# Delta-rule solve: one direction's diagonal blocks made by VectorE transposes, one direction's far half evicted by VectorE, ScalarE's copies reordered

## The chip, the cores and the metric

One core of one Trainium2 chip runs the whole program. The metric is the device time of one execution in microseconds (us), lower is better.

## The reference, cut to what matters

The program is one inference step of a two-layer hybrid backbone: SwiGLU blocks and, between them, a token mixer of attention heads, RWKV-7 heads and retention heads. The change touches the RWKV-7 part alone: a scan over tokens in two directions, four heads of width 64, with a generalised delta rule:

```python
def rwkv7_scan(r, w, kk, kka, k, v, s0):
    def step(S, inp):
        r_t, w_t, kk_t, kka_t, k_t, v_t = inp
        sa = jnp.einsum('bzhvk,bzhk->bzhv', S, -kk_t)
        S = S * w_t[..., None, :] + sa[..., None] * kka_t[..., None, :] + v_t[..., None] * k_t[..., None, :]
        return S, jnp.einsum('bzhvk,bzhk->bzhv', S, r_t)
```

There are 512 latent tokens (started from a given state) and 128 context tokens (started from zero).

## The kernel before, in words

All tokens (640) stand in five chunks of 128: chunks 0 to 3 are latent, chunk 4 (`last`, `c == NL`) is the context. The scan of a chunk is turned into a triangular system per head and direction, and `solve(c)` solves it. Both directions (d = 0 and 1) and four heads go side by side. Each layer runs `solve(0)` to `solve(4)`, so there are ten solves in the program, eight of them not the last of their layer.

A solve inverts the 128x128 unit triangle in steps. First its four 32x32 diagonal blocks: `horner` and three `levels` work on compact tiles `Xc[d]` (128 partitions x 4 heads x 32 columns: block q of every head lies on partitions 32q to 32q+31) and on `XTc[d]`, the same with each 32x32 block transposed (L2062, VectorE). Then the pairs of 32-blocks: TensorE multiplies for the off-diagonal blocks (L1677, whose result ScalarE copies out as `T1` in L1918, then L1687, semaphore `dx_mm` with count 5c+4). The 64x64 diagonal triangles are then put together in `XT[d]` (128 x 4 heads x 128), which holds the transposed inverse, from two sources: the diagonal 32x32 blocks out of `XTc` (direction 0: ScalarE, `diagonal`, L1891; direction 1: VectorE, L2140, four copies of 32 partitions x 128 elements each) and the off-diagonal blocks, transposed out of PSUM by VectorE for both directions (L2148, two for direction 0, then two for direction 1). TensorE then multiplies `XT[d]` with the right-hand sides `R` (L1455, eight matmuls in each direction); half of `R` is the values, which ScalarE copies from PSUM in `values_out` (L1876, semaphore `lv`). ScalarE copies the result to `X` (L1929). The other half of the triangle follows: TensorE forms its product with the near half (L1710, semaphore `t1_mm` with count 5c+5), the product is copied from PSUM to `Zs[d]` (L1936: both directions on ScalarE, 64 partitions x 512 elements each), TensorE multiplies it (L1722, semaphore `gh_mm`), and VectorE adds it to `X` (L2163).

The order of the work on each engine is written out by hand, and the parts of the next chunk's preparation, `prep(c+1, 0)` to `prep(c+1, 4)`, are put between the steps of the solve. Each engine takes its own list in order, and waits on semaphores. Around the change the orders in a chunk that is not the last are:

- TensorE: L1677, `lk_values(c, 0)` (L1461), L1687, `lk_values(c, 1)` (L1461), L1455, `prep(c+1, 2)` (transposes L1407 and L1408, waiting for `alpha` and `kappa`), L1710, `prep(c+1, 3)` (transposes L1416 to L1419, which wait for `beta` and `rk` before the first of them), L1722, then `inner(c+1, 0, d)` (L1448), then the final products of chunk c.
- VectorE: the last level, L2140, L2148, `prep(c+1, 2)` (L2008 to L2011, gives `alpha`), `prep(c+1, 3)` (L2014 to L2025, gives `rho`, `beta` and `rk`), `prep(c+1, 4)` (L2036 to L2040, waits for `tok_T`, which the last of L1419 gives), L2163.
- ScalarE: `T1` twice (L1918), `values_out(c, 0)`, `diagonal(c)` (L1891), `values_out(c, 1)`, `X` twice (L1929), `Zs` twice (L1936), `prep(c+1, 3)` (L1819, L1822, wait for `tok_T`).
- GpSimd: four masks and the products of the preparation (L2262, L2251), with no step of its own in this stretch.

TensorE's `inner(c+1, 0, d)` waits for what `prep(c+1, 4)` of VectorE and `prep(c+1, 3)` of ScalarE put out (`beta_tok`, `v_tok`, `bv`, `alpha_tok`, `kappa_tok`).

In the last chunk there is no preparation; in its place `beside(...)` does the group norm and gate of earlier tokens: VectorE has `beside(3)`, `beside(4)`, `beside(5)` between L2148 and L2163, ScalarE has `beside(3)` between `diagonal` and `X`, `beside(4)` between `X` and `Zs`, and TensorE `beside(3)` ahead of L1455, `beside(4)` ahead of L1710, `beside(5)` ahead of L1722.

The semaphore of `t10` and `t11` (counts of `T1`, `X` and `Zs` of direction 0 and 1, six each in a chunk) is one for both directions, counted in turn:

```python
series("level_lx_out", 30, "t10", "t11")
```

Of the kernel before, what the change touches and what calls it, by code (L numbers as in the profile page):

```python
# [22 lines left out]
ACT = mybir.ActivationFunctionType  # L23
AX = mybir.AxisListType.X

P = 128
# [73 lines left out]
def flip(c):  # L100

    return 4 * (c % 2)
# [33 lines left out]
def build(nc, i, o):  # L136
    ctx = ExitStack()
    with ctx:
# [70 lines left out]
        PS = ctx.enter_context(nc.psum_tensor("PS", [P, 8, 512], F32))  # L209
# [113 lines left out]
        class Stage:  # L323
# [6 lines left out]
            def value(self, l, k):  # L330
# [103 lines left out]
        XT = [keep(f"XT{d}", [P, NH, P], rq) for d in range(2)]  # L434
# [3 lines left out]
        Zs = [keep(f"Zs{d}", [P, NH, P], fo) for d in range(2)]  # L438
# [15 lines left out]
        Xc, T1, XTc = ([place(f"{one}{d}", [P, NH, QUAD], at_lvl + 4 * P * (7 * d + at)) for d in range(2)]  # L454
                       for at, one in ((2, "Xc"), (3, "T1_"), (4, "XTc")))
# [10 lines left out]
        S = {}  # L466

        def stage(name, per):
            S[name] = Stage(ctx.enter_context(nc.semaphore(name)), per)

        def series(name, per, *names):
            s_ = ctx.enter_context(nc.semaphore(name))
            for turn, one in enumerate(names):
                S[one] = Stage(s_, per, turn, len(names))
# [52 lines left out]
        series("horner", 15, "b_mm0", "b_mm1")  # L527
        series("lak_v", 5, "lv0", "lv1")
        series("level_lx", 25, "t1_mm0", "t1_mm1")
        series("level_lx_out", 30, "t10", "t11")  # L530
        series("solve_results", 5, "gh_mm0", "gh_mm1", "fin_mm0", "fin_mm1", "yl_mm0", "yl_mm1")
        series("gh_out", 5, "gh0", "gh1")
        series("yl", 5, "yl_out0", "yl_out1")
# [10 lines left out]
        def until(eng, l, name, k):  # L544

            if S[name].per * l + k > 0:
                eng.wait_ge(S[name].sem, S[name].value(l, k))
# [1277 lines left out]
        def rwkv_scalar(a_, l):  # L1825
            until(a_, l, "pv", 40)
            until(a_, l, "s_mm", 40)
            until(a_, l, "mix_stored", 48)

            def prep(c, part):  # L1830

                prep_scalar(a_, l, c, part)

            def beside(lv):

                t = lv - 2
                if 0 <= t < NL:
                    gn_square(a_, l, NT + t)
                    gate_copy(a_, l, t, 0)
                if 0 <= t < 3:  # L1840
                    until(a_, l, "cols_T", t + 1)
                    if t == 0:
                        until(a_, l, "tok_T", 5)
                        until(a_, l, "rk", 5)
                        until(a_, l, "kd", 5)
                    cols = slice(t * P, (t + 1) * P)
                    a_.activation(act[0][:, 0:4, cols], PS[:, 2, :].rearrange("p (k t) -> p k t", k=4), ACT.Copy)
                    a_.activation(act[0][:, 6:8, cols], PS[:, 3, 0:256].rearrange("p (k t) -> p k t", k=2), ACT.Copy)\
                        .then_inc(S["cols_out"].sem, 1)
                if lv > 4:  # L1850
                    rwkv_columns(a_, l, lv - 5)

            def rows_out(c):

                for d in range(2):
                    until(a_, l, f"lb_mm{d}", c + 1)
                    until(a_, l, f"yl_mm{d}", max(c - 1, 0))
                    for pr in range(2):
                        m = a_.activation(LB[c % 2][d][:, pr:NH:2, :, :],
                                          PS[:, (4 + 2 * d + pr) ^ flip(c), :].rearrange("p (f e t) -> p f e t", f=2, e=2),  # L1860
                                          ACT.Copy)
                    m.then_inc(S[f"lb{d}"].sem, 1)

            def key_rows_out(c, d):

                until(a_, l, f"lk_mm{d}", c + 1)
                until(a_, l, f"yl_mm{d}", c)
                for pr in range(2):
                    m = a_.activation(LK[d][:, pr:NH:2, :, :],
                                      PS[:, (2 * d + pr) ^ flip(c), :].rearrange("p (f e t) -> p f e t", f=2, e=2), ACT.Copy)  # L1870
                m.then_inc(S[f"lko{d}"].sem, 1)

            def values_out(c, d):

                until(a_, l, f"lv_mm{d}", c + 1)
                a_.activation(R[c % 2][d][:, :, HD:P], PS[:, (2 + d) ^ flip(c), 0:DR].rearrange("p (h v) -> p h v", h=NH),  # L1876
                              ACT.Copy).then_inc(S[f"lv{d}"].sem, 1)

            def local_out(c, d):

                until(a_, l, f"yl_mm{d}", c + 1)
                a_.activation(Yls[:, c, d * DR:(d + 1) * DR], PS[:, (5 + 2 * d) ^ flip(c), 0:DR], ACT.Copy)\
                    .then_inc(S[f"yl_out{d}"].sem, 1)

            def diagonal(c):

                until(a_, l, "x0", 10 * c + 10)
                until(a_, l, "gh_mm0", c)
                for q in range(4):
                    at = slice(q * QUAD, (q + 1) * QUAD)  # L1890
                    m = a_.activation(XT[0][at, :, at], XTc[0][at, :, :], ACT.Copy)  # L1891
                m.then_inc(S["xt0"].sem, 1)

            def solve(c):
                f, last = flip(c), c == NL
                rows_out(c)
                if c == 0:
                    prep(0, 3)
                else:
                    local_out(c - 1, 0)  # L1900
                if not last:
                    prep(c + 1, 0)
                if c:
                    local_out(c - 1, 1)
                key_rows_out(c, 0)
                key_rows_out(c, 1)
                if not last:
                    prep(c + 1, 1)
                    prep(c + 1, 2)
                else:  # L1910
                    values_out(c, 0)
                    values_out(c, 1)
                    beside(1)
                    beside(2)
                for d in range(2):
                    until(a_, l, f"t1_mm{d}", 5 * c + 4)
                    until(a_, l, f"dx_mm{d}", 5 * c + 3)
                    a_.activation(T1[d][:].rearrange("p h t -> p (h t)"), PS[:, (4 + 2 * d) ^ f, 0:P], ACT.Copy)\  # L1918
                        .then_inc(S[f"t1{d}"].sem, 1)
                if not last:  # L1920
                    values_out(c, 0)
                diagonal(c)
                if last:
                    beside(3)
                else:
                    values_out(c, 1)
                for d in range(2):
                    until(a_, l, f"dx_mm{d}", 5 * c + 5)
                    a_.activation(X[d][:].rearrange("p h t -> p (h t)"), PS[:, (5 + 2 * d) ^ f, :], ACT.Copy)\  # L1929
                        .then_inc(S[f"t1{d}"].sem, 1)  # L1930
                if last:
                    beside(4)
                for d in range(2):
                    until(a_, l, f"t1_mm{d}", 5 * c + 5)
                    b = slice(64, P) if d == 0 else slice(0, 64)
                    a_.activation(Zs[d][b, :, :].rearrange("p h t -> p (h t)"), PS[b, (4 + 2 * d) ^ f, :], ACT.Copy)\  # L1936
                        .then_inc(S[f"t1{d}"].sem, 1)
                if last:
                    beside(5)
                    beside(6)  # L1940
                    local_out(c, 0)
                    local_out(c, 1)
                else:
                    prep(c + 1, 3)

            for c in range(NT):
                solve(c)
            rwkv_columns(a_, l, 2)
# [96 lines left out]
        def rwkv_vector(v_, l):  # L2045
            mm_ = lambda name, k: until(v_, l, name, k)
# [3 lines left out]
            def prep(c, part):  # L2050

                prep_vector(v_, l, c, part)
# [47 lines left out]
            def solve(c):  # L2100
                last = c == NL
# [35 lines left out]
                mm_("x1", 10 * c + 10)  # L2137
                for q in range(4):
                    at = slice(q * QUAD, (q + 1) * QUAD)
                    m = v_.tensor_copy(XT[1][at, :, at], XTc[1][at, :, :])  # L2140
                m.then_inc(S["xt1"].sem, 1)
                for d in range(2):
                    mm_(f"dx_mm{d}", 5 * c + 4)
# [6 lines left out]
                if last:  # L2150
                    beside(3)
                    beside(4)
                    beside(5)
                else:
                    prep(c + 1, 2)
                    prep(c + 1, 3)
                    prep(c + 1, 4)
                for d in range(2):
# [10 lines left out]
            def beside(lv):  # L2169

                if lv >= 3:
                    rwkv_gate(v_, l, lv - 3)
                if 2 <= lv <= 5:
                    gn_squares(v_, l, NT + lv - 2)
                if lv <= NL:
                    rwkv_centre(v_, l, lv - 1)
# [1073 lines left out]
```

## Time and profile before

| | us |
|---|---|
| median of 3 runs | 3168.57 |
| lowest and highest of them | 3167.96, 3171.4 |
| the profiled execution's own time | 3171.75 |
| its span in the profile | 3169.9 |
| TensorE busy | 3023.3 (95%) |
| VectorE busy | 1830.3 (58%) |
| ScalarE busy | 1078.5 (34%) |
| GpSimd busy | 412.2 (13%) |
| mean granted TensorE clock | 0.974 |

The mixer's ten solves lie in two stretches of the span, from 866 to 1057 us (layer 0) and from 2397 to 2613 us (layer 1). In the rows, a time is the start in us from the span's start, the next number how long it lasted; PE is TensorE's matmuls, PEld its weight loads, DVE VectorE, ACT ScalarE, POOL GpSimd, PS the PSUM; L and a number is the line of the kernel. The text in square brackets is the time that the engine sat idle before, and what ended it.

### The profile page before, as it was taken

The numbers are of one execution on the slowest core, as the hardware profiler recorded it, in microseconds if no ns is written. First come the engines' busy times: TensorE is split into PE (matmuls) and PEld (weight loads), VectorE is DVE, ScalarE is ACT, GpSimd is POOL, SyncE is SP. The second block draws the span as 40 slices with busy tenths as digits, with TensorE's granted clock in tenths as the row PEclk, the third lists the DMA queues.
The fourth block names the chain that finished last, engine by engine and source line by source line (L and its number), as shares of the span: only waits on it lengthen the run. The fifth ranks groups of instructions, "written<-read, shape, count | busy, mean of one in ns | idle before, by whom it ended". The sixth has DMA issues, their size and how long they took to land.

```text
span 3169.9 us, 62838 instructions
## 1 busy us (share of the span) xinstructions
PE 3023.3 (95%) x26760; PEld 2713.3 (86%) x26760; DVE 1830.3 (58%) x2648; ACT 1078.5 (34%) x1619; POOL 412.2 (13%) x465
## 2 busy tenths in 40 slices
PE   6999999999988899999999999999998879999998
PEld 5999978986777699998799998789776767999986
DVE  3767555666766666674656674633666676222235
ACT  3111254235433441113531113532454435211134
POOL 1000111002233220001100001110033233000100
PEclk8999999999899899999999999999998989999999
DMA  5344334311000233433433433432010003111134
GB/s 221 133 159 159 119 134 147 123 41 33 24 3 13 102 119 146 159 146 120 146 137 141 159 146 124 143 106 83 17 47 7 7 24 140 67 72 74 60 125 167
DMA packets 62635, 324.09 MB, mean 102 GB/s; under 512 B 8752, under 2 KB 12400, under 8 KB 42992
## 3 DMA queue, kind: packets, MB, share of 16 engines
q1 hardware_dynamic: 62448, 321.39, 27.7%
q8 instruction: 143, 2.34, 0.3%
q14 instruction: 44, 0.36, 0.0%
HBM read 318.05 MB, written 3.31 MB: 101 GB/s over the span
## 4 chain that ended last, share of the span: by engine, by line
PE 84%; DVE 7%; DMA 3%; ACT 2%; issue 2%; POOL 0%; SPq 0%; ACTq 0%; DVEq 0%; POOLq 0%
PE PS L2464 47%; PE PS L2547 17%; PE PS L2475 3%; DMA wo<-in_wo 2%; PE PS L695 2%; PE PS L1469 2%; DVE wo_lo L2864 1%; PE PS L719 1%; ACT wo_hi L2661 1%; PE PS L1448 1%; PE PS L1455 1%; PE PS L642 1%; DMA wm<-in_wm 1%; PE PS L707 1%; PE PS L1461 1%
## 5 line engine op out<-in xcount | busy, mean ns | idle before, releaser
L2464 PE MATMUL PS<-h_hi,wi_hi 128*128 128x384 f32 (+1 forms) x3360 | 799.7, 310 | 11.0 <-issue 11.0
L2464 PE MATMUL PS<-h_lo,wi_hi 128*128 128x384 f32 (+1 forms) x3360 | 797.7, 309 | 0.0
L2464 PE MATMUL PS<-h_hi,wi_lo 128*128 128x384 f32 (+1 forms) x3360 | 797.7, 309 | 0.0
L2464 PEld LDWEIGHTS PS<-h_hi,wi_hi 128*128 128x128 f32 x3360 | 526.6, 188 | 14.0 <-issue 13.2
L2464 PEld LDWEIGHTS PS<-h_lo,wi_hi 128*128 128x128 f32 x3360 | 526.4, 188 | 0.7
L2464 PEld LDWEIGHTS PS<-h_hi,wi_lo 128*128 128x128 f32 x3360 | 526.4, 188 | 0.7
L2547 PE MATMUL PS<-wo_hi,a_hi 128*128 128x512 f32 x968 | 394.5, 408 | 21.7 <-DVE wo_lo L2864 14.6
L2864 DVE TENSOR_TENSOR wo_lo<-wo,wo_hi 128x1024 fp32r<-128x1024 f32 x208 | 256.1, 1232 | 259.5 <-ACT wo_hi L2661 258.5
L2654 ACT ACTIVATE sg<-PS 128x640 f32<-128x640 f32 x88 | 62.2, 706 | 937.5 <-PE PS L2464 937.5
L2547 PE MATMUL PS<-wo_lo,a_hi 128*128 128x512 f32 x968 | 378.9, 391 | 0.0
L2547 PE MATMUL PS<-wo_hi,a_lo 128*128 128x512 f32 x968 | 378.7, 391 | 0.0
L2290 DVE SCALAR_TENSOR_TENSOR macc<-wm,csil,macc 128x512 f32<-128x512 f32 x448 | 337.0, 752 | 15.9
L2661 ACT ACTIVATE wo_hi<-wo 128x1024 fp32r<-128x1024 f32 x208 | 220.3, 1059 | 342.2 <-PE PS L2547 226.9
L2858 DVE TENSOR_TENSOR act<-sg,PS 128x256 f32 (+3 forms) x176 | 78.0, 485 | 431.8 <-ACT sg L2654 431.8
L2850 DVE TENSOR_TENSOR wi_lo<-wi,wi_hi 128x2048 fp32r<-128x2048 f32 x112 | 256.4, 2290 | 79.5 <-ACT wi_hi L2648 79.3
L2547 PEld LDWEIGHTS PS<-wo_hi,a_hi 128*128 128x128 f32 x968 | 182.3, 188 | 84.6 <-DVE wo_lo L2864 34.4
L2648 ACT ACTIVATE wi_hi<-wi 128x2048 fp32r<-128x2048 f32 x112 | 213.5, 1906 | 11.4 <-DMA wi<-in_wi 8.7
L2547 PEld LDWEIGHTS PS<-wo_lo,a_hi 128*128 128x128 f32 x968 | 182.7, 189 | 39.4 <-issue 4.8
L2547 PEld LDWEIGHTS PS<-wo_hi,a_lo 128*128 128x128 f32 x968 | 182.6, 189 | 39.2
L3050 POOL TENSOR_TENSOR gcol<-modc,ngc 128x16 f32<-128x16 f32 x6 | 2.5, 412 | 1199.6 <-PE PS L2464 594.8
L2872 DVE TENSOR_TENSOR a_lo<-act,a_hi 128x512 fp32r<-128x512 f32 (+1 forms) x98 | 79.4, 811 | 43.7 <-ACT a_hi L2678 43.7
L3024 POOL TENSOR_SCALAR stat<-stat 128x1 f32<-128x1 f32 x60 | 24.8, 414 | 614.0 <-ACT PS L2684 576.0
(323 smaller groups left out, 3841.1 us busy)
## 6 DMA issues: line engine op xcount, KB each, us to landing
wi<-in_wi SPq DMA_DIRECT2D x88, 1024.0 KB, 4.9
wo<-in_wo SPq DMA_DIRECT2D x176, 512.0 KB, 3.5
wm<-in_wm SPq DMA_DIRECT2D x36, 2048.0 KB, 7.4
wi<-in_win SPq DMA_DIRECT2D x24, 1024.0 KB, 5.2
wo<-in_wout SPq DMA_DIRECT2D x32, 512.0 KB, 3.5
wq<-in_wq SPq DMA_DIRECT2D x2, 1024.0 KB, 4.8
out_y_sample<-x SPq DMA_DIRECT2D x4, 512.0 KB, 4.7
lvl<-in_lvl SPq DMA_DIRECT2D x2, 896.0 KB, 6.0
```

The source lines that it names most:

```text
L695: mm = pe.matmul(dst, q, KT[0:96, h, a:z], start=True, stop=True)
L1469: mm = pe.matmul(PS[at, bank, h * QUAD:(h + 1) * QUAD], lhs(h, at), rhs(h, at), start=True, stop=True)
L2290: a = dve.scalar_tensor_tensor(out=macc[:, z, :], in0=w[:, k, :], scalar=csil[:, k, z:z + 1], in1=macc[:, z, :], op0=ALU.mult, op1=ALU.add)
L2464: mm = pe.matmul(PSF[0:cols, at:at + GW[g]], st, h[g][:, k, :], start=(k == 0 and q == 0), stop=(k == KD - 1 and q == 2))
L2475: mm = pe.matmul(PS[:, 3 * j + t // 2, (t % 2) * 256:(t % 2 + 1) * 256], h[g][:, k, at], w[:, j, k, :], start=(k == 0 and q == 0), stop=(k ...
L2547: mm = pe.matmul(PS[:, OUT_BANK[t] + half, :], a, w[:, (V0(n) + b) % 2, kk, :], start=(u == 0 and kk == 0 and q == 0), stop=True, skip_gro ...
L2648: act_.activation(wi_hi[:, j, :, :], wi[:, j, :, :], ACT.Copy).then_inc(s_wih, 1)
L2661: act_.activation(wo_hi[:, V % 2, :, :], wo[:, V % 2, :, :], ACT.Copy).then_inc(s_woh, 1)
L2850: dve.tensor_tensor(wi_lo[:, j, :, :], wi[:, j, :, :], wi_hi[:, j, :, :].bitcast(F32), ALU.subtract).then_inc(s_wil, 1)
L2858: a = dve.tensor_tensor(tile_at(act[g], f), sg[:, j, GA[g]:GA[g] + GW[g]], PSF[:, up:up + GW[g]], ALU.mult)
L2864: dve.tensor_tensor(wo_lo[:, V % 2, :, :], wo[:, V % 2, :, :], wo_hi[:, V % 2, :, :].bitcast(F32), ALU.subtract).then_inc(s_wol, 1)
L2872: dve.tensor_tensor(act_lo(g, A, b == 0), act[g][:, 2 * u:2 * u + 2, :], act_hi(g, A, b == 0).bitcast(F32), ALU.subtract).then_inc(s_al, 1)
```

## The change

Three edits. VectorE's four copies `XTc[1]` to `XT[1]` become four transposes of `Xc[1]` to `XT[1]` (a 32x32 block transpose gives the same blocks). The eviction of the product to `Zs[1]` goes from ScalarE to VectorE, where it stands behind `prep(c+1, 2)` and ahead of `prep(c+1, 3)`, with a wait for `t1_mm1` (in the last chunk behind `beside(4)` and ahead of `beside(5)`); `t10` and `t11` get a semaphore each. On ScalarE `values_out(c, 0)` goes behind `diagonal(c)` in chunks that are not the last.

```diff
@@ -527,7 +527,8 @@
-        series("level_lx_out", 30, "t10", "t11")
+        stage("t10", 30)
+        stage("t11", 30)
@@ -1917,12 +1918,11 @@
                     a_.activation(T1[d][:].rearrange("p h t -> p (h t)"), PS[:, (4 + 2 * d) ^ f, 0:P], ACT.Copy)\
                         .then_inc(S[f"t1{d}"].sem, 1)
-                if not last:
-                    values_out(c, 0)
                 diagonal(c)
                 if last:
                     beside(3)
                 else:
+                    values_out(c, 0)
                     values_out(c, 1)
@@ -1930,11 +1930,9 @@
                 if last:
                     beside(4)
-                for d in range(2):
-                    until(a_, l, f"t1_mm{d}", 5 * c + 5)
-                    b = slice(64, P) if d == 0 else slice(0, 64)
-                    a_.activation(Zs[d][b, :, :].rearrange("p h t -> p (h t)"), PS[b, (4 + 2 * d) ^ f, :], ACT.Copy)\
-                        .then_inc(S[f"t1{d}"].sem, 1)
+                until(a_, l, "t1_mm0", 5 * c + 5)
+                a_.activation(Zs[0][64:P, :, :].rearrange("p h t -> p (h t)"), PS[64:P, 4 ^ f, :], ACT.Copy)\
+                    .then_inc(S["t10"].sem, 1)
@@ -2137,7 +2135,7 @@
                 mm_("x1", 10 * c + 10)
                 for q in range(4):
                     at = slice(q * QUAD, (q + 1) * QUAD)
-                    m = v_.tensor_copy(XT[1][at, :, at], XTc[1][at, :, :])
+                    m = v_.transpose(XT[1][at, :, at], Xc[1][at, :, :])
                 m.then_inc(S["xt1"].sem, 1)
@@ -2150,9 +2148,15 @@
                 if last:
                     beside(3)
                     beside(4)
+                else:
+                    prep(c + 1, 2)
+                mm_("t1_mm1", 5 * c + 5)
+                mm_("gh_mm1", c)
+                v_.tensor_copy(Zs[1][0:64, :, :].rearrange("p h t -> p (h t)"), PS[0:64, 6 ^ flip(c), :])\
+                    .then_inc(S["t11"].sem, 1)
+                if last:
                     beside(5)
                 else:
-                    prep(c + 1, 2)
                     prep(c + 1, 3)
                     prep(c + 1, 4)
```

## Rows read from the trace of the kernel before

**Rows 1.** The page: busy share of each engine, and the chain that ended last.
```profile
PE 3023.3 (95%) x26760; PEld 2713.3 (86%) x26760; DVE 1830.3 (58%) x2648; ACT 1078.5 (34%) x1619; POOL 412.2 (13%) x465
...
PE 84%; DVE 7%; DMA 3%; ACT 2%; issue 2%; POOL 0%; SPq 0%; ACTq 0%; DVEq 0%; POOLq 0%
```
**Rows 2.** Longest pieces of that chain within 866 to 1090 us: start, us, what.
```profile
919.87 1.21 DVE XT L2140
922.05 3.13 PE PS L1455 x16
...
927.63 0.59 PE PS L1416 x4
...
930.61 2.00 PE PS L1448 x16
```
**Rows 3.** Timeline of VectorE in chunk 1 of layer 0.
```profile
917.29 0.31 DVE L2062 STREAM_TRANSPOSE XTc<-Xc 128x128 f32<-128x128 f32 x1
...
918.23 3.10 DVE L2140 COPY XT<-XTc 32x128 f32<-32x128 f32 x4
921.35 1.30 DVE L2148 STREAM_TRANSPOSE XT<-PS 32x128 f32<-32x128 f32 x4
...
923.57 0.68 DVE L2014 TENSOR_TENSOR E<-E,rwz 128x512 f32<-128x512 f32 x1
...
925.58 0.61 DVE L2025 SCALAR_TENSOR_TENSOR rk<-rk,mcol,rwz 128x128 f32<-128x128 f32 x2
928.77 0.69 DVE L2036 COPY btok<-PS 128x512 f32<-128x512 f32 x1 [2.58 <-PE PS L1419]
929.38 0.41 DVE L2038 COPY vtok<-PS 128x256 f32<-128x256 f32 x1
```
**Rows 4.** Timeline of GpSimd in the same chunk.
```profile
916.04 2.50 POOL L2262 TENSOR_TENSOR LB<-LB,mask 128x512 f32<-128x512 f32 x2
918.49 2.51 POOL L2262 TENSOR_TENSOR LK<-LK,mask 128x512 f32<-128x512 f32 x2
```
**Rows 5.** Instructions on the tile XT: ns min/median/max; below, who waited (us, times).
```profile
L2140 DVE COPY XT<-XTc x40: 206/864/1220, 882.2 to 2588.2; 32x128 f32<-32x128 f32 x40
...
  PE PS L1455: 16.0, 7
```
**Rows 6.** Timeline of TensorE in the same chunk.
```profile
919.34 0.69 PE L1461 MATMUL PS<-vtok,LK 128*64 128x64 f32 x16
922.05 3.13 PE L1455 MATMUL PS<-R,XT 128*128 128x128 f32 x16 [2.02 <-DVE XT L2148]
...
927.57 0.66 PE L1416 MATMUL PS<-ident,ab 128*128 128x128 f32 x4
```
**Rows 7.** Timeline of ScalarE in the same chunk.
```profile
918.32 0.28 ACT L1918 ACTIVATE T<-PS 128x128 f32<-128x128 f32 x1 [0.24 <-PE PS L1677]
...
919.21 1.25 ACT L1891 ACTIVATE XT<-XTc 32x128 f32<-32x128 f32 x4
920.48 0.38 ACT L1876 ACTIVATE R<-PS 128x256 f32<-128x256 f32 x1
...
927.67 1.21 ACT L1936 ACTIVATE Zs<-PS 64x512 f32<-64x512 f32 x2 [1.85 <-PE PS L1710]
```
**Rows 8.** Stretches of 2 us: busy us of each engine; PEclk is the third number from the end.
```profile
922.00:924.00 2.00, 1.95 (x12) 1.96 (x13) 1.90 (x6) 0.49 (x1) 0.00 (x0) 0.70 0.00 0
924.00:926.00 2.00, 2.00 (x11) 2.00 (x11) 1.89 (x5) 0.70 (x2) 0.00 (x0) 0.50 0.00 0
926.00:928.00 2.00, 2.00 (x25) 1.66 (x24) 0.19 (x1) 0.33 (x1) 0.00 (x0) 0.95 0.00 0
```
**Rows 9.** Timeline of VectorE in the last chunk of layer 0.
```profile
1043.41 0.75 DVE L2202 TENSOR_TENSOR Yls<-Yls,PS 128x256 f32<-128x256 f32 x2 [1.58 <-PE PS L1747]
...
1045.73 0.68 DVE L1049 TENSOR_TENSOR yc<-yc,gst 128x512 f32<-128x512 f32 x1
...
1048.88 1.40 DVE L2163 TENSOR_TENSOR X<-X,PS 64x512 f32<-64x512 f32 x2
```

## The prediction

> **What bounds the kernel now.** I read the page first: TensorE is busy for 95% of the span, and the chain that ended last is 84% TensorE and 7% VectorE [rows 1]. That says only that work off this chain is free, so I next read the chain inside the solves [rows 2]. There VectorE's copies into `XT` (L2140) stand on the chain right ahead of TensorE's L1455, and from L1455 on the chain stays on TensorE: L1407/L1408, L1710, and, without a gap, L1416. So two places count: what TensorE waits for at L1455, and what it would wait for at L1416.
>
> At L1455 the view of instructions on the tile gives the size: TensorE waited 16.0 us in 7 of the ten solves for `XT` [rows 5]. The timelines of chunk 1 tell why. TensorE's L1461 started at 919.34 and its 0.69 us end at 920.03; L1455 starts at 922.05 after 2.02 idle [rows 6]. VectorE took 3.10 us for four copies of 32 x 128, and only then came to L2148 [rows 3]. One such copy takes 0.21 us at best, 0.86 in the median, 1.22 at worst [rows 5], and GpSimd was at its masks, 1.25 us each, from 916.04 to 921.00 [rows 4]. The worst copy is about one mask long: the copies are held up beside GpSimd. A VectorE transpose of 128 x 128 at 917.29, beside the same masks, took 0.31 [rows 3, 4]. The Trainium skill (GPSIMD Engine Reference, Specifications) says that GpSimd shares its SBUF interface with VectorE instructions that run in a two-port mode or read two SBUF inputs; by that a plain fp32 copy is exposed and a transpose need not be, and the trace agrees (0.86 against 0.31).
>
> **Part 1, transposes for copies.** Four transposes of 32 partitions out of PSUM take 1.30 us, 0.33 from start to start [rows 3]. With an SBUF source the nearest row is 0.31. Ends: 1.30, if that holds; 3.10, if these are held up like the copies. I take 1.3. In chunk 1: transposes from 918.23 to 919.5, then L2148, whose direction 0 (two transposes) is done at about 920.2.
>
> **Part 2, ScalarE's order.** L1455 of direction 0 also waits for `values_out(c, 0)`. Its new place is behind `diagonal`: the second `T1` starts at 918.32, `diagonal` follows at about 918.6 and takes 1.25, then `values_out` 0.38 [rows 7], done at 920.25. That is beside VectorE's 920.2, so L1455 can start at 920.3 in place of 922.05. Of the 2.02 idle some 0.2 to 0.3 stays. Over the seven waits: 16.0 minus 7 x 0.2 is **14.6 us gained**, all in chunks that are not the last (the eighth of them had no wait there: TensorE itself came late).
>
> **Part 3, the eviction on VectorE.** This adds a wait to VectorE, and I ask what is queued behind it. VectorE's `prep(c+1, 3)` runs from L2014 at 923.57 to the end of L2025 at 926.19: 2.62 us [rows 3]. TensorE's L1416 needs `beta` and `rk`, which these give, and starts at 927.57 [rows 6]: before, they were ready 1.4 us early. Now VectorE waits for L1710 first, evicts, and only then starts them. And L1710 is the step right ahead of L1416 on TensorE; L1722, which uses `Zs`, is queued behind L1416. So TensorE must wait, once L1710 is done, for
> - the hand-over to VectorE, 0.04 (L1710 ended at 927.63 [rows 2], ScalarE's copy started at 927.67 [rows 7]);
> - the eviction. Nearest rows: a PSUM copy of 128 x 512 on VectorE, 0.69 with the next starting 0.61 later [rows 3]; ScalarE needs 1.21 for two [rows 7]. I take 0.61;
> - `prep(c+1, 3)`: 2.62;
> - the hand-over to TensorE, 0.1.
>
> Together 3.37 us in each of eight chunks, **27.0 us lost**. ScalarE's second eviction, 0.6 us, goes, but it hid behind TensorE's transposes: L1722 saves about 0.2, yet the chain from `tok_T` to L1448 goes over VectorE's L2036 to L2040, which keep their distance from L1419. Nothing is gained there. GpSimd has no part in this stretch, and no DMA issue is moved. Separate semaphores for `t10` and `t11` change no wait that is last: nothing.
>
> **Last chunks.** L1455 there is queued behind `beside(3)` and does not wait for `XT`. GpSimd's masks are over by then, so I take the shortest copy of rows 5, 0.21, against 0.31: the transposes cost VectorE 0.4 more; the later idle of 1.58 [rows 9] takes that up. The eviction stands on VectorE ahead of the instruction at 1045.73, from where it goes on without a pause to L2163 at 1048.88 [rows 9], which TensorE's last products await: plus 0.61 in each layer, **1.2 us lost**.
>
> **TensorE's clock.** After the 2.02 idle the granted clock was 0.70, then 0.50, then 0.95 in three stretches of 2 us [rows 8]: full speed is 2.4 GHz, 0.50 is 1.2. The lost part is 0.6 + 1.0 + 0.1 = 1.7 us at most. The idle ahead of L1455 goes, so this price may go too: 0 to 1.7 in each of eight chunks, up to 13.6. The new idle of 3.3 us ahead of L1416 is longer and lies behind a busy stretch, so I expect the same fall there: the same 0 to 1.7 each, less what falls into the 1.8 us from L2036 to L1448 [rows 2, 3], when TensorE waits for VectorE. I let the two cancel. The Trainium skill (TensorE: Matmul & The Clock Gate, Why this matters for your kernels) warns that an idle gap between bursts takes the clock to its lower level; by that rule the change moves the gap and lengthens it, and does not free the clock. The trace agrees that a gap of 2.02 us was followed by 0.50.
>
> **Sum.** 27.0 + 1.2 - 14.6 + 0 = **+13.6 us**. The terms are made against the profiled execution, 3171.75 us (span 3169.9 and 1.9 around it), which gives 3185.3. That execution stands 3.2 above the median of the runs, 3168.57; against the median I predict **3182 us**, 0.43% slower. A measurement of this kernel can tell about 0.2%, 6.3 us, from no change.
>
> **Rivals.**
> - *The clock comes back.* The half-speed stretch goes together with the gap at L1455 and does not appear after the new one. Up to 13.6 less: 3168 to 3175, no change. For it: the fall of rows 8 sat right behind that gap. Against: the new gap is longer. 0.14.
> - *The clock costs twice.* The new gap costs its full 1.7 and the low speed at L1455 stays, from gaps further ahead. Up to +13.6 more, and some 8 likely: 3190. 0.12.
> - *Transposes are held up like copies.* Then the 14.6 is not gained, +28: 3197. Against: 0.31 beside the masks. 0.04.
> - *L1416 does not wait* (the other side). If `beta` and `rk` are ready by the time L1710 is done, the 27.0 falls away and -14.6 + 1.2 leaves 3155. It decides at L1416: this holds only if VectorE puts them out less than about 1.8 us after L1710 (the mean gain of part 1 over eight chunks), where the rows give 3.3. It would need the eviction to wait for something earlier, or the order of `prep(c+1, 3)` to be other than the diff says. 0.04.
>
> **How the numbers follow.** The forecast has 0.66. Slower: forecast (0.62 of its 0.66), clock twice, held-up transposes, 0.79 together. No change: the clock coming back and a small part of the forecast, 0.16. Faster: 0.05, L1416's case and a sliver of the clock's. The range 3172 to 3191 takes in the clock's bounds on both sides of 3182 and leaves out the far rivals and the tails of the near ones.
>
> **What the profile would show.** Right: L2140 as transposes of about 0.31 with no mark of GpSimd; idle ahead of L1455 at most 0.4 us; a new idle of about 3.3 us ahead of L1416, released by VectorE's L2025 (`rk`), eight times; a 0.6 us copy to `Zs` on VectorE right behind L1710. Wrong: L1416 with no idle ahead, or transposes of 0.8 us. If the total is off with those steps right, it is the clock: the granted clock in the stretches from L1455 to L1448 will tell.

## The result, and the profile after

| | before | after |
|---|---|---|
| median of the runs (us) | 3172.07 (6 runs, 3167.96 to 3175.55) | 3192.77 (6 runs, 3190.22 to 3195.28) |
| profiled execution (us) | 3171.75 | 3193.48 |
| its span (us) | 3169.9 | 3191.7 |
| granted TensorE clock over the span | 0.974 | 0.969 |

The change makes the kernel slower: ratio 1.0065, 95% interval [1.0054, 1.0075], or 20.7 us by the medians. I predicted 13.6 us slower (3182, range 3172 to 3191). The 3182 was counted from the median of the three runs that I had, 3168.57; six runs of the same kernel gave 3172.07. So of the 10.6 us between 3182.2 and 3192.8, 3.5 come from where I started to count and 7.1 from the change (20.7 against 13.6). Between the two profiled executions the difference is 21.7 us. All ratios are of fast runs; one of the eleven runs of "The new gap filled" took 7464.71 us and is left out of its ratio.

I went through the profile after in the order of the prediction. First the instructions on the tile `XT` (ns min/median/max, then who waited, in us, and how often), after:

```profile
L2138 DVE STREAM_TRANSPOSE XT<-Xc x40: 292/302/308, 883.5 to 2610.2; 32x128 f32<-32x128 f32 x40
L2146 DVE STREAM_TRANSPOSE XT<-PS x40: 305/312/323, 884.8 to 2611.5; 32x128 f32<-32x128 f32 x40
...
  PEld PS L1456: 2.2, 6
  PE PS L1456: 1.3, 5
```

The transposes take 0.30 us with almost no spread, where the copies took 0.21 to 1.22 [rows 5], and TensorE's wait for `XT` fell from 16.0 us to 1.3. (L1456 is the L1455 of before: the lines have moved by one.) Then VectorE's timeline in chunk 1 of layer 0, which answers to [rows 3]:

```profile
918.97 1.25 DVE L2138 STREAM_TRANSPOSE XT<-Xc 32x128 f32<-32x128 f32 x4
920.25 1.31 DVE L2146 STREAM_TRANSPOSE XT<-PS 32x128 f32<-32x128 f32 x4
...
921.87 0.69 DVE L2009 TENSOR_TENSOR E<-E,kk 128x512 f32<-128x512 f32 x1
925.03 0.68 DVE L2155 COPY Zs<-PS 64x512 f32<-64x512 f32 x1 [2.47 <-PE PS L1711]
925.63 0.67 DVE L2012 TENSOR_TENSOR E<-E,rwz 128x512 f32<-128x512 f32 x1
...
927.63 0.61 DVE L2023 SCALAR_TENSOR_TENSOR rk<-rk,mcol,rwz 128x128 f32<-128x128 f32 x2
930.47 0.69 DVE L2034 COPY btok<-PS 128x512 f32<-128x512 f32 x1 [2.23 <-PE PS L1420]
```

VectorE now stands idle for 2.47 us in front of the eviction (L2155), waiting for L1711, with the whole of `prep(c+1, 3)` queued behind it. And TensorE in the same chunk, which answers to [rows 6]:

```profile
921.04 2.02 PE L1456 MATMUL PS<-R,XT 128*128 128x128 f32 x16 [0.26 <-DVE XT L2146]
...
923.86 1.09 PE L1711 MATMUL PS<-X,LB 64*64 64x128 f32 x16
928.38 1.09 PE L1417 MATMUL PS<-ident,ab 128*128 128x128 f32 x4 [3.43 <-DVE rk L2023]
...
930.36 1.97 PE L1723 MATMUL PS<-Zs,XT 64*64 64x128 f32 x16
932.31 2.98 PE L1449 MATMUL PS<-E,ab 64*128 64x256 f32 x16
```

The wait ahead of L1456 is 0.26 where it was 2.02, and there is a new one of 3.43 ahead of L1417 (the L1416 of before), in all eight chunks, released by `rk`. The waits are those forecast. What is not: the durations. L1456 takes 2.02 us where it took 3.13 [rows 6], but L1417 takes 1.09 for 0.66, and L1449 2.98 where it took 2.00 [rows 2]. The view of 2 us stretches, PEclk third from the end, shows why:

```profile
922.00:924.00 2.00, 2.00 (x20) 1.83 (x20) 0.56 (x1) 1.20 (x2) 0.00 (x0) 1.00 0.03 8
924.00:926.00 2.00, 0.95 (x16) 0.71 (x14) 0.97 (x2) 0.59 (x1) 0.00 (x0) 1.00 0.00 0
926.00:928.00 2.00, 0.00 (x0) 0.00 (x0) 1.89 (x5) 0.00 (x0) 0.00 (x0) 0.88 0.00 0
928.00:930.00 2.00, 1.62 (x8) 1.65 (x9) 0.24 (x1) 0.00 (x0) 0.00 (x0) 0.50 0.00 0
930.00:932.00 2.00, 2.00 (x19) 1.91 (x18) 1.44 (x3) 1.15 (x3) 0.00 (x0) 0.50 0.00 0
932.00:934.00 2.00, 2.00 (x12) 1.56 (x10) 1.37 (x2) 0.00 (x0) 0.00 (x0) 0.50 0.00 0
```

Behind the old gap the clock was 0.70 and 0.50 for two stretches, then 0.95 [rows 8]. Behind the new one it is 0.50 for three. Chunk 1 is one of the dearer chunks: L1417 took 0.63 to 1.09 us over the eight, so at times the clock fell only after it; L1723 took 1.9 to 2.0 in each (L1722 took 1.09 before), and L1449 took 2.00 in two chunks, as before, and 2.5 us or more in the others.

To add it up I took the two stretches of the solves, each from the first L1448 (L1449) to the first products of the output stage for later tokens. Before, then after; the first number is the length, the second TensorE's busy time, PEclk third from the end:

```profile
861.80:1069.20 207.40, 175.73 (x4721) 150.76 (x4721) 135.17 (x354) 79.03 (x178) 62.85 (x61) 0.89 0.08 28
2421.30:2625.60 204.30, 175.13 (x4719) 150.15 (x4720) 134.34 (x354) 78.95 (x178) 62.74 (x61) 0.88 0.08 28
sum 411.70, PE 350.86 PEld 300.91 DVE 269.51 ACT 157.98 POOL 125.59; mean PE 175.43 PEld 150.46 DVE 134.75 ACT 78.99 POOL 62.80
```

```profile
863.20:1080.60 217.40, 182.46 (x4721) 155.84 (x4721) 131.23 (x359) 76.64 (x173) 62.85 (x61) 0.84 0.07 27
2432.60:2648.90 216.30, 180.93 (x4720) 155.77 (x4721) 130.97 (x359) 76.73 (x173) 62.80 (x61) 0.85 0.08 27
sum 433.70, PE 363.39 PEld 311.61 DVE 262.19 ACT 153.37 POOL 125.65; mean PE 181.69 PEld 155.81 DVE 131.10 ACT 76.68 POOL 62.83
```

All of the loss lies here: 411.7 to 433.7, 22.0 us. TensorE ran the same number of matmuls (4720 or so in each stretch) and was busy 12.5 us longer (350.9 to 363.4); its idle time (length less busy) rose by 9.5 (60.8 to 70.3). The granted clock is down from 0.89 and 0.88 to 0.84 and 0.85. More busy time for the same work is clock.

### The profile page after: what moved, and what is told of

It reads as the page before. It is cut to its first block, busy times and chain, and to the rows that moved or that the text cites. A ratio compares the mean times of both kernels' runs of the same rounds, so it can differ in the third digit from the quotient of the medians.

```text
span 3191.7 us, 62823 instructions
## 1 busy us (share of the span) xinstructions
PE 3039.4 (95%) x26760; PEld 2728.1 (85%) x26760; DVE 1823.3 (57%) x2658; ACT 1073.8 (34%) x1609; POOL 412.2 (13%) x465
## 4 chain that ended last, share of the span: by engine, by line
PE 84%; DVE 7%; DMA 3%; ACT 2%; issue 2%; POOL 0%; SPq 0%; DVEq 0%; ACTq 0%; POOLq 0%
PE PS L2468 46%; PE PS L2551 17%; PE PS L2479 3%; DMA wo<-in_wo 2%; PE PS L696 2%; PE PS L1470 2%; DVE wo_lo L2868 1%; PE PS L1449 1%; ACT wo_hi L2665 1%; PE PS L720 1%; PE PS L1462 1%; PE PS L643 1%; PE PS L708 1%; PE PS L1393 1%; PE PS L2517 1%
## 5 line engine op out<-in xcount | busy, mean ns | idle before, releaser
L2551 PE MATMUL PS<-wo_hi,a_hi 128*128 128x512 f32 x968 | 393.3, 406 | 21.3 <-DVE wo_lo L2868 13.7
```

The costliest lines, as they stand in the source:

```text
L2551: mm = pe.matmul(PS[:, OUT_BANK[t] + half, :], a, w[:, (V0(n) + b) % 2, kk, :], start=(u == 0 and kk == 0 and q == 0), stop=True, skip_gro ...
```

## The experiments

Each run is compared by its ratio to runs of the kernel before on the same chip and at the same time, since the median of before lay between 3172 and 3177 us from one set of runs to the next. One hundredth of the ratio is 31.7 us.

### The new gap filled

```diff
                 if last:
                     beside(5)
                 else:
+                    for _ in range(3):
+                        pe.matmul(PS[:, side_bank(c + 1, 1), :], ident[:], R[c % 2][0][:].rearrange("p h t -> p (h t)"),
+                                  start=True, stop=True)
                     prep(c + 1, 3)
```

> The changed kernel, and in each of the eight chunks that are not the last TensorE runs three extra matmuls (identity times a 128 x 512 tile) between L1710 and L1416, into a bank that L1416 writes over afterwards. Three take about 2.6 us at full speed, less than the 3.43 us that TensorE stands idle there. My theory is that what the waits don't explain of the loss (20.7 measured, 13.2 from waits) is TensorE's lower clock behind this idle: then the granted clock stays at 1.00 from L1416 to L1448 and the time falls by 6 to 14 us against the changed kernel, to some 3179 to 3187, still slower than before. Rival, the last chunk's eviction costs more than I reckoned: then the filling changes nothing, 3190 to 3196, or adds a little.

Measured: 3178.66 us, ratio 1.0018 [1.0009, 1.0027]. Against 1.0065 without the filling, 0.0047 less: 15 us are gained by giving TensorE more work. The timeline of TensorE in chunk 1 shows that the order of things is the same:

```profile
924.84 1.09 PE L1711 MATMUL PS<-X,LB 64*64 64x128 f32 x16
925.86 2.84 PE L1719 MATMUL PS<-R,ident 128*128 128x512 f32 x6
929.37 0.63 PE L1417 MATMUL PS<-ident,ab 128*128 128x128 f32 x4 [0.66 <-DVE rk L2026]
```

From the start of L1711 to that of L1417 it is 4.53 us, as in the changed kernel (4.52): the wait for `rk` ends no earlier. But L1417 takes 0.63, not 1.09, and the stretches of 2 us behind it have PEclk 1.00:

```profile
930.00:932.00 2.00, 1.53 (x22) 1.27 (x21) 1.42 (x3) 1.15 (x3) 0.00 (x0) 1.00 0.00 0
932.00:934.00 2.00, 1.61 (x15) 1.62 (x16) 1.39 (x3) 0.44 (x1) 0.00 (x0) 1.00 0.00 0
```

So the price of the new gap is its own length and, on top, some 15 us of lower clock, 1.9 for each of the eight chunks if it is shared out among them (in the profiled executions some of it lies in the last chunks, see below). By the Trainium skill (TensorE: Matmul & The Clock Gate, Why this matters for your kernels) an idle gap between bursts takes the clock down; the runs agree, and they also show low clock with no such gap right ahead (see the transposes alone).

### The last chunks undone

```diff
-                until(a_, l, "t1_mm0", 5 * c + 5)
-                a_.activation(Zs[0][64:P, :, :].rearrange("p h t -> p (h t)"), PS[64:P, 4 ^ f, :], ACT.Copy)\
-                    .then_inc(S["t10"].sem, 1)
+                for d in range(2 if last else 1):
+                    until(a_, l, f"t1_mm{d}", 5 * c + 5)
+                    b = slice(64, P) if d == 0 else slice(0, 64)
+                    a_.activation(Zs[d][b, :, :].rearrange("p h t -> p (h t)"), PS[b, (4 + 2 * d) ^ f, :], ACT.Copy)\
+                        .then_inc(S[f"t1{d}"].sem, 1)
```

(and VectorE's wait and copy only where `not last`)

> The changed kernel with the eviction of direction 1 given back to ScalarE in the last chunk of each layer alone. Theory of the clock: VectorE's 0.6 us in each layer go, 1.2 us in all, and the time is 3190 to 3193. Rival, the last chunk is dear: the stretch from the last L1448 to the output products was 5.5 and 2.5 us longer in the two layers; if that is the eviction, the time falls by 8, to about 3185.

Measured: 3195.61 us, ratio 1.0075 [1.0061, 1.0089], against 1.0065 [1.0054, 1.0075]. The 8 us are not there; whether the 1.2 us are, this can't tell. The growth of the last chunks isn't that of the eviction. The stretch from the last L1448 (L1449) to the output stage, in both layers, before and then after (PEclk third from the end):

```profile
1011.29:1069.20 57.91, 45.97 (x795) 38.51 (x791) 39.32 (x94) 18.91 (x41) 16.51 (x17) 0.79 0.20 77
2569.28:2625.60 56.32, 43.26 (x793) 35.96 (x790) 39.60 (x95) 18.84 (x41) 16.80 (x17) 0.85 0.21 78
```

```profile
1016.87:1080.60 63.73, 50.90 (x795) 43.12 (x791) 40.32 (x96) 18.64 (x40) 16.86 (x17) 0.68 0.18 70
2590.50:2648.90 58.40, 44.75 (x794) 38.00 (x791) 40.37 (x95) 18.61 (x40) 16.74 (x17) 0.80 0.20 76
```

Together 114.2 became 122.1, 7.9 of the 22.0 us; TensorE was busy 6.4 us longer with the same matmuls, at a lower clock. What lowered it there isn't shown. The same stretches took 118.4 us in the kernel with the new gap filled and 117.1 in this one, each in a single execution, so part of the 7.9 may be chance.

### The transposes and ScalarE's order, without the eviction

> The kernel before with two of the three edits: transposes for VectorE's copies, and ScalarE's new order; both evictions stay on ScalarE (each direction with its own semaphore). Waits alone: the idle ahead of L1455 falls from 16.0 to about 1.8 us, 14 us faster than before, about 3158. Theory of the clock: the half-speed stretch behind that idle goes too, at 1.0 to 1.7 us in six chunks, so 20 to 24 us faster, about 3148 to 3152. L1416 has no idle ahead of it.

The edit is the change less its hunks on `Zs`. Measured: 3153.61 us, ratio 0.9938 [0.9924, 0.9952]: 19.7 us faster than before. The same two stretches, in this kernel:

```profile
863.40:1060.70 197.30, 171.75 (x4721) 148.11 (x4721) 127.20 (x354) 79.29 (x178) 62.89 (x61) 0.90 0.09 29
2412.40:2608.40 196.00, 168.86 (x4719) 144.62 (x4720) 127.86 (x354) 79.28 (x178) 62.81 (x61) 0.91 0.09 29
sum 393.30, PE 340.61 PEld 292.74 DVE 255.06 ACT 158.57 POOL 125.70; mean PE 170.31 PEld 146.37 DVE 127.53 ACT 79.28 POOL 62.85
```

393.3 us against 411.7: idle 52.7 (8.1 less) and busy 340.6 (10.3 less). The number lies between the two that I had written down (14 us faster by the waits alone, 20 to 24 with the clock). The waits that I priced at 14.6 are thus not the whole of it; the clock gives some 5 us more, net of new waits that a faster L1456 opens. I had written that L1416 would have no idle ahead of it. That was a miss: with L1456 faster TensorE comes to it early, and it waits 0.29 or 0.51 us for `rk` in some chunks:

```profile
958.08 0.63 PE L1417 MATMUL PS<-ident,ab 128*128 128x128 f32 x4 [0.51 <-DVE rk L2025]
```

The low clock at L1456 did not go everywhere with the gap. In four of the eight chunks of this kernel, and in two of the changed kernel, L1456 still took 2.4 to 3.8 us with no idle shown ahead of it, and in all six the products ahead of it (L1462, 0.69 at full clock, 1.12 here) were already slow. In the kernel before it was so in the one chunk in which L1455 did not wait. From chunk 0 of layer 0, the transposes alone:

```profile
885.50 1.12 PE L1462 MATMUL PS<-vtok,LK 128*64 128x64 f32 x16
886.55 3.78 PE L1456 MATMUL PS<-R,XT 128*128 128x128 f32 x16
```

So a gap right ahead isn't the only thing behind which the clock is low; what else lowers it here, no run shows.

### The eviction alone

> The kernel before with the third edit alone: the eviction of direction 1 on VectorE, the copies of before and ScalarE's order of before. Idle ahead of L1416 3.4 us in eight chunks, 27.4, and 1.2 in the last chunks: 28.6 us slower, about 3201, if the clock is neutral. Theory of the clock: both gaps now have a half-speed stretch behind them, 8 to 14 us more, about 3209 to 3215.

The edit is the change's hunks on `Zs` and on the semaphores, with the copies and ScalarE's order of before. Measured: 3224.37 us, ratio 1.0162 [1.0148, 1.0176], 51.4 us slower. That is more than either number that I had written down. Both gaps are open, each with its low clock behind it, as TensorE's timeline in chunk 1 shows:

```profile
926.49 3.78 PE L1456 MATMUL PS<-R,XT 128*128 128x128 f32 x16 [2.01 <-DVE XT L2147]
931.90 1.27 PE L1711 MATMUL PS<-X,LB 64*64 64x128 f32 x16
936.61 1.09 PE L1417 MATMUL PS<-ident,ab 128*128 128x128 f32 x4 [3.44 <-DVE rk L2024]
938.60 1.97 PE L1723 MATMUL PS<-Zs,XT 64*64 64x128 f32 x16
940.54 2.97 PE L1449 MATMUL PS<-E,ab 64*128 64x256 f32 x16
```

### Both gaps filled

To that kernel, the three matmuls of the first experiment and two more ahead of L1455:

```diff
                 else:
                     lk_values(c, 1)
+                    until(pe, l, "p_inv", c + 2)
+                    for _ in range(2):
+                        pe.matmul(PS[:, side_bank(c + 1, 1), :], ident[:], E[c % 2][:, 0].rearrange("p f e t -> p (f e t)"),
+                                  start=True, stop=True)
```

> The kernel with the eviction alone (52 us slower than before, both gaps open), with extra matmuls in both gaps: two ahead of L1455, three ahead of L1416. The waits stay as they are, 28.6 us more than before. If the clock made the rest of the 52, the time falls to about 3172 + 28.6 less what the filling of the first gap alone gave (9): 3190 to 3202. Rival, the eviction on VectorE costs over 28.6 in some other way: it stays above 3210.

Measured: 3195.35 us, ratio 1.0068 [1.0052, 1.0083], in place of 1.0162. Filling took back 0.0094, 30 of the 51 us, and the time is in the range that I had written down. What is left is 21.6 us. The waits (28.6) less what filling the old gap alone gave (next experiment: 10.5, interval 6.7 to 14.6) would leave 14 to 22: it fits, near the upper end. Within that, the eviction costs what its wait and the lower clock cost.

### The old gap filled, in the kernel before

The two matmuls ahead of L1455 alone, in the kernel before.

> The kernel before, with two extra matmuls (identity times 128 x 512) on TensorE between the last L1461 and L1455 in chunks that are not the last, into a bank that is written over later. Two take 1.7 us at full speed, less than the 2.0 to 2.6 us of idle there. Theory of the clock: the fall behind that idle goes and the time falls by 5 to 10 us, to 3162 to 3167, though the wait itself stays. Rival, the clock is set by something else: no change, or some us slower, where the extra matmuls run at half speed.

Measured: 3167.57 us, ratio 0.9967 [0.9954, 0.9979]: 10.5 us faster. The low clock at L1455 cost the kernel before about that much, 1.3 us for each of eight chunks. TensorE in chunk 1:

```profile
924.64 1.95 PE L1455 MATMUL PS<-R,XT 128*128 128x128 f32 x16
927.39 1.09 PE L1714 MATMUL PS<-X,LB 64*64 64x128 f32 x16
```

L1455 takes 1.95 us, not 3.13 [rows 6]. The price is rather too low: in three of the eight chunks the clock was low before the added matmuls began, they took longer (3.45 us in chunk 1) and L1455 followed them without idle, later than VectorE would have let it start.

### A third of the new gap filled

One matmul in place of three.

> The changed kernel with one extra matmul in place of three in the new gap: about 0.9 us of 3.4 filled, 2.5 idle, like the gaps of 2.0 to 2.6 us in the kernel before, behind which the clock fell. Theory: the fall stays, 3188 to 3194. Rival, any work in the gap is enough, or the matmul's power and not the idle counts: 3179 as with three.

Measured: 3192.64 us, ratio 1.0049 [1.0031, 1.0067]. The interval overlaps that of the changed kernel (from 1.0054 up) and stays clear of three matmuls (up to 1.0027). So one is not enough for the whole cure; whether it cures a part isn't settled. The median hides that the twelve runs fall apart in two groups: four took 3175 to 3180 us, like the kernel with three matmuls, and eight 3186 to 3199, while all six runs of the changed kernel took over 3190.

### GpSimd's masks held back, in the kernel before

```diff
+                if c + 1 < NT:
+                    until(po, l, "xt1", 2 * c + 1)
                 for d in range(2):
                     masked(c, "lko", LK[d], 1, d).then_inc(S[f"lkm{d}"].sem, 1)
```

> The kernel before with one wait added on GpSimd: in chunks that are not the last, its last two masks of LK wait until VectorE's four copies to XT are done; the copies stay copies. My theory is that the copies are long because they are held up beside GpSimd. Then they take about 0.21 us each, 1.0 to 1.3 us for four, the idle ahead of L1455 shrinks from 16.0 us to under 3, and the time falls much as with the transposes (3153.6), to 3150 to 3160. Rival, the copies are slow by themselves (32 partitions, a strided target): no change, 3168 to 3176.

Measured: 3158.58 us, ratio 0.9949 [0.9935, 0.9963], 16 us faster with one wait added on GpSimd and nothing changed on VectorE. The tile view and GpSimd's and VectorE's rows in chunk 1:

```profile
L2140 DVE COPY XT<-XTc x40: 207/219/1034, 884.4 to 2569.5; 32x128 f32<-32x128 f32 x40
```

```profile
915.13 2.50 POOL L2262 TENSOR_TENSOR LB<-LB,mask 128x512 f32<-128x512 f32 x2
918.48 2.50 POOL L2262 TENSOR_TENSOR LK<-LK,mask 128x512 f32<-128x512 f32 x2 [0.86 <-DVE XT L2140]
```

```profile
917.30 1.10 DVE L2140 COPY XT<-XTc 32x128 f32<-32x128 f32 x4
918.43 1.31 DVE L2148 STREAM_TRANSPOSE XT<-PS 32x128 f32<-32x128 f32 x4
```

The median copy falls from 864 to 219 ns; what still meets the first pair of masks (up to 917.63) keeps its 1 us at most. The copies were not slow by themselves, they were held up beside GpSimd.

### The eviction behind prep(c+1, 3)

VectorE's wait and copy one place later (they are taken out of their place ahead of `prep(c + 1, 3)`), and ScalarE's in the last chunks:

```diff
                 else:
                     prep(c + 1, 2)
                     prep(c + 1, 3)
+                    mm_("t1_mm1", 5 * c + 5)
+                    mm_("gh_mm1", c)
+                    v_.tensor_copy(Zs[1][0:64, :, :].rearrange("p h t -> p (h t)"), PS[0:64, 6 ^ flip(c), :])\
+                        .then_inc(S["t11"].sem, 1)
                     prep(c + 1, 4)
```

> The changed kernel with VectorE's eviction one place later in chunks that are not the last, behind prep(c+1, 3) and ahead of prep(c+1, 4), and on ScalarE in the last chunks. My theory is that only what was queued behind the new wait made the loss: then L1416 has an idle of at most 0.5 us ahead of it, and the time is that of the transposes alone, 3153.6, within 3. L1722 no longer waits 0.28 for Zs, which TensorE gives back at L1448. Rival, VectorE's eviction itself costs: a gap ahead of L1448 grows by 0.6 us in eight chunks, 5 us slower than the transposes alone.

Measured: 3156.96 us, ratio 0.9939 [0.9925, 0.9952], the same as the transposes alone (0.9938). The instruction is the same; one place in the order of VectorE's list is worth 0.0126, 40 us (the last chunks, which this kernel also gives back, had no measurable share above). The wait ahead of L1417 is at most 0.67 us.

### ScalarE's old order

> The transposes alone, with ScalarE's order of before: values_out(c, 0) ahead of diagonal. I took ScalarE's part for a tie: either order ends at the same time, since L1455 of direction 0 waits for both. Then 3153.6 within 3. Rival, the old order holds L1455 back: values_out(c, 0) waits for L1461 (0.34 us idle in the kernel before) and pushes diagonal behind it, so L1455 waits up to 0.4 us more in eight chunks: 3 us slower.

Measured: 3155.45 us, ratio 0.9929 [0.9912, 0.9946], against 0.9938 [0.9924, 0.9952]. No difference: the reordering of ScalarE's copies is worth nothing that can be measured.

## Why the prediction was wrong

Point by point, by its own steps.

**Part 1** held: four transposes in 1.25 us (1.3 forecast), and 1.3 us in place of 16.0 waited for `XT`, 14.7 less; the gain of 14.6 was the right size for the wait. The cause, GpSimd, was argued there and is now shown by the masks held back.

**Part 2** held: a tie, and the two orders can't be told apart.

**Part 3** held to a tenth: 3.43 us in each of eight chunks, 3.37 forecast; released by `rk`, as forecast. That it was the order and not the eviction is shown by the kernel with the eviction behind `prep(c+1, 3)`.

**Last chunks.** From L2202 to L2163 it was 5.47 us [rows 9]. After the change, with these lines moved by four, it is

```profile
1052.06 0.75 DVE L2206 TENSOR_TENSOR Yls<-Yls,PS 128x256 f32<-128x256 f32 x2 [2.07 <-PE PS L1748]
...
1058.12 1.40 DVE L2167 TENSOR_TENSOR X<-X,PS 64x512 f32<-64x512 f32 x2
```

6.06: the 0.6 of the forecast. Undoing it gained nothing that could be measured.

**TensorE's clock: this step failed.** I let the gain at the old gap and the loss at the new one cancel, each bounded at 0 to 1.7 us per chunk, and so put the term at 0. With the waits as measured, 27.4 + 1.2 - 14.7 is 13.9; the 20.7 measured leaves some 7 us for the clock.

That low clock costs this much is shown by the fillings, in the kernels in which each gap is open: 10.5 us at the old gap (1.3 per chunk), 15 at the new one (1.9, a little over the bound). Nor did the change give the 10.5 back whole: the transposes alone were 19.7 us faster, 5 more than the 14.6 of waits, and L1456 was still slow in two of the changed kernel's eight chunks. By these prices 15 less 5, 10 us, had been put at nought, and 13.6 + 10 = 23.6 stands to 20.7 measured: the direction and the size are right, the sum is not exact.

The bound was read from one stretch of one gap [rows 8], in which low clock covered L1455 and then ended. Behind the longer gap low clock lasted over L1417, L1723 and, in most chunks, L1449, and part of these I had wrongly taken as hidden beside VectorE. The last chunks, too, I had priced without a word on the clock.

Where the 7 us arise stays open. In the two profiled executions 14.1 of the 22.0 us lie in the chunks that are not the last, where the waits alone make 12.7, so that the two clock terms nearly cancel there; the other 7.9 lie in the last chunks, where the eviction explains 1.2. One execution of each kernel can't say how much of this is the rule.

The rival "the clock costs twice", with its 3190, came nearest in number. Its first half was right, the new gap's full price; its second half, low speed that stays at L1455, held in two chunks of eight.

The terms can't be summed more finely than this. At low clock TensorE is busy in time in which it would otherwise wait, so that idle rose by 9.5 where the waits alone said 14.

## What to carry to other kernels

Before a wait goes into an in-order engine's list, list what stands behind it and who needs that: the same copy one place later was worth 40 us here. Price an idle gap on TensorE as its length plus the work that follows at half speed, about half as much again here (1.9 us behind 3.4, 1.3 behind 1.5 to 2.6), and check it by filling the gap with matmuls whose result nobody reads. Look in the trace that they end before the wait does: at low clock they can run over it. Count low clock per chunk, before and after, and not in one chunk only. When one instruction's time jumps between 0.21 and 1.2 us, look at GpSimd's timeline beside it before replacing it; a wait on GpSimd may do.

## What had not been expected of the hardware

- Extra matmuls made kernels faster: three per chunk 15 us, two per chunk 10.5 us, both sets 30 us. L1455 took up to 3.79 us in chunks with the old gap open ahead of it, 1.95 to 2.05 with it filled.
- The costs of two gaps add up to more than each alone: 51.4 us for the eviction with the old gap open, where on top of the transposes it costs 0.0127, 40 us. TensorE's busy time in the two stretches was 381.1 us for the same matmuls that took 340.6 with the transposes alone:

```profile
sum 464.30, PE 381.10 PEld 327.20 DVE 275.52 ACT 153.81 POOL 125.74; mean PE 190.55 PEld 163.60 DVE 137.76 ACT 76.91 POOL 62.87
```

- VectorE's transposes of SBUF tiles (0.30 us for 32 x 128) ran beside GpSimd's two-input masks without being held up, copies of the same size did not.
